# A gate table in device memory, laid out by table position or by chunk of the down stage

## The chip, the cores and the metric

The kernel runs on one core of a Trainium2 chip, as one launch. The metric is the time of the launch on the device in microseconds (us), lower is better. In this text PE is the matrix engine, DVE the vector engine, ACT the scalar engine, POOL the GpSimd engine and SP the engine that only issues transfers. "PEld" in a row is PE's weight load, and "SPq" and "ACTq" are the queues of instructions of SP and ACT. A core has 16 DMA engines, which move what all queues issue.

## What is computed

One layer of a hybrid block over 512 positions of width 1024 in float32: an attention branch and a short convolution, then a retrieval over 128 x 128 = 16384 experts of one neuron each (`peer_ffn`), then a norm. The change is in the experts.

```python
top_s, top_i = lax.top_k(s, 16)                       # per head and half: 16 of 128 keys
cand_s = top_s[:, :, 0, :, None] + top_s[:, :, 1, None, :]
cand_i = top_i[:, :, 0, :, None] * 128 + top_i[:, :, 1, None, :]
best_s, best_c = lax.top_k(cand_s, 16)                # 16 of 256 pairs, 8 heads
gate = jax.nn.softmax(best_s, axis=-1)
act = gelu(einsum('nhkd,nd->nhk', expert_u[expert_idx], x))
return einsum('nhk,nhkd->nd', gate * act, expert_v[expert_idx])
```

Each token picks 128 experts. An expert's number is i * 128 + j.

## The kernel before

The 512 tokens are four blocks of 128. Three of them (384 tokens) are computed densely: every expert's activation for every token is worked out, and multiplied by a gate that is zero unless the token picked the expert. The fourth ("sparse") block is computed by fetching the picked rows. On the way from one to the other there are two tables in device memory: `expert_act` (name `hd`) with the activations, i x j x 384 tokens, and `expert_gate` (name `gd`) with the gates, in 12 batches of 32 tokens.

**Up stage**, about 500 to 1215 us, 128 steps, one for each j, of some 5.5 us. In step n PE transposes the next 128 rows of `expert_u` (line 1144) and multiplies the rows of step n (24 matmuls, line 1154) in three passes over high and low halves: ACT copies the high half `uh` out of PSUM (1238), DVE takes the low half `ul` (1412), and PE needs both for the next step. ACT then runs the gelu and writes the activations of the step to `expert_act` from its own queue (1245, 1247). The raw rows of `expert_u` stand in four buffers; SP issues the load for a buffer when its transposes are done, four steps ahead of its next use (1073).

The gates are built beside it, in three blocks of 16 groups of 8 tokens. DVE makes one-hot rows (`hot`, 1475 and 1477), ACT multiplies by the gates' high part (1269), POOL makes the low part (1381), PE multiplies the one-hots into a table of gates in PSUM (`spread`, 1181), ACT evacuates it into one of two buffers `parts` (`evac`, 1279), and POOL adds the two halves of `parts` into `grid` (`gather`, 1390). Eight such additions fill the grid, 128 keys x 32 tokens. SP then writes it to the gate table (`send`, 1084), 12 times in all, four in a block. POOL's next addition waits for the send to have landed, since there is one grid; ACT's evacuation waits for the addition of two before, since there are two `parts`.

The sparse block runs here too: POOL issues an indirect DMA for each of 128 picked rows of `expert_u` (`fetch`, 1371) into a ring of five buffers, and DVE multiplies each with the tokens (`row`, 1487), between the other tasks of a step. A table by step says how many rows DVE takes, and POOL fetches as ring buffers are freed. DVE, ACT and POOL each run a fixed order, so that a wait in front of one task holds what stands behind it.

**Down stage**, about 1220 to 1742 us, 32 chunks of four j each. For a chunk SP loads 2 MB of `expert_v` (1076), 768 KB of activations (`dh`, 1088) and 768 KB of gates (`dg`, 1091); DVE multiplies the two (1512), ACT and DVE split everything into high and low halves (1286, 1295, 1496, 1505), and PE does 72 matmuls (1213). Buffers are double, and the loads of a chunk are issued when the chunk two before has been split. DVE also adds the fetched rows of `expert_v` for the sparse block (1492). The first gate read waits until all 12 sends have landed.

Of the kernel before, what the change touches and what calls it, by code (L numbers as in the profile page):

```python
# [18 lines left out]
F = mybir.dt.float32  # L19
# [7 lines left out]
P = 128  # L27
# [10 lines left out]
KEYS = 128  # L38
# [28 lines left out]
DT = DB * P  # L67
# [849 lines left out]
G4 = 4  # L917
ROUNDS = KEYS // G4 // 2
# [74 lines left out]
def experts_program(nc, sem, psum, m, a, acc, sT, const, score, rank_of, gain, st, hd, gd, raw, u_in, u_view, ut_full, shared, out):  # L993
# [10 lines left out]
    grid = m.put("grid", 112, [P, KEYS, 32])  # L1004
# [21 lines left out]
    dg = [m.put(f"dg{i}", kb, [P, DT // 32, G4, 32]) for i, kb in enumerate((150, 174))]  # L1026
# [18 lines left out]
    S = {n: sem(n) for n in (  # L1045
        "v_half eq_hot eq_key found index_ready exp_in exp_out gate_norm sel_ready selT_full selT_in gate_split hot_eq "
        "g_evac g_sum g_out x3_ready row_used dot_act weighed").split()}
    v_part = [sem(f"v_part{i}") for i in range(2)]
    row_in = [sem(f"row_in{i}") for i in range(RING_D)]
    v_in, dg_in, dh_in, v_hi, v_lo, w_f, w_hi, w_lo, mm_done = (  # L1050
        [sem(f"d_{n}{i}") for i in range(2)] for n in ("v_in", "g_in", "h_in", "v_hi", "v_lo", "w_f", "w_hi", "w_lo", "mm_done"))
# [3 lines left out]
    uv = u_view.rearrange("i (r s) d -> i r s d", s=4)  # L1055
    vv = a["expert_v"][0].rearrange("(i r j) d -> i r (j d)", r=KEYS // G4, j=G4)
    hg = hd.rearrange("i (r j) t -> i r (j t)", j=G4)
    gv = gd.rearrange("b i (r x) -> i b r x", x=G4 * 32)
    HALF = STEPS // 2
    ORDER = {SPARSE: 0, 0: 1, 1: 2, 2: 3}  # L1060

    def experts_sync(sp_):

        for free in (*ut_full, *u_mm, *h_done, *g_full, S["g_evac"], S["g_sum"], *v_lo, *w_lo):
            sp_.sem_inc(free, PRIMED)
        for free in (*h_out, S["g_out"]):
            sp_.sem_inc(free, PRIMED * 16)

        def load(r, buffers=range(4)):
            for s in buffers:  # L1070

                sp_.wait_ge(ut_full[s % 2], r * 2 + s // 2)
                sp_.dma_start(raw[s][:].unsqueeze(1), uv[:, ds(r, 1), s, :]).then_inc(u_in[s], 16)

        def load_rows(s, at):
            sp_.dma_start(v_raw[s][:].rearrange("p j d -> p (j d)").unsqueeze(1), vv[:, at, :]).then_inc(v_in[s], 16)

        def load_part(s, j):
            sp_.dma_start(v_raw[s][:, j:j + 1, :], vv[:, s:s + 1, j * D:(j + 1) * D]).then_inc(v_part[s], 16)

        def send(q):

            sp_.wait_ge(S["g_sum"], 8 * q + 8 + PRIMED)
            sp_.dma_start(gd[:, :, :].rearrange("b p x -> p b x")[:, q:q + 1, :],
                          grid[:].rearrange("p j n -> p (j n)").unsqueeze(1)).then_inc(S["g_out"], 16)

        def load_acts(s, at):
            sp_.dma_start(dh[s][:].rearrange("p j t -> p (j t)").unsqueeze(1), hg[:, at, :]).then_inc(dh_in[s], 16)

        def load_gates(s, at):  # L1090
            sp_.dma_start(dg[s][:].rearrange("p b j n -> p b (j n)"),
                          gv[:, :, at, :].rearrange("p b o x -> p b (o x)")).then_inc(dg_in[s], 16)

        sp_.wait_ge(last_tile, tiles)
        load(0, range(3, 4))
        for r in range(1, STEPS // 4):
            load(r, range(2))
            if 4 * r - 4 in SEND:
                send(SEND[4 * r - 4])
            load(r, range(2, 4))  # L1100
            if r in AHEAD_AT:
                i = AHEAD_AT.index(r)
                if i in (0, G4):
                    sp_.wait_ge(ranked, EACH * (12 + i))
                elif i == G4 + 2:
                    sp_.wait_ge(S["selT_full"], DB)
                load_part(*divmod(i, G4))
        load_acts(0, slice(0, 1))

        sp_.wait_ge(S["g_out"], (DT // 32 + PRIMED) * 16)  # L1110
        load_gates(0, slice(0, 1))

        for s in range(2):
            sp_.wait_ge(ut_full[s], HALF + PRIMED)
        load_acts(1, slice(1, 2))
        load_gates(1, slice(1, 2))

        for s in range(2):
            sp_.wait_ge(h_out[s], (HALF + PRIMED) * 16)
        with sp_.Fori(1, ROUNDS) as r:  # L1120
            for s in range(2):

                sp_.wait_ge(w_lo[s], r + PRIMED)
                load_acts(s, ds(r * 2 + s, 1))
                load_gates(s, ds(r * 2 + s, 1))
                sp_.wait_ge(v_lo[s], r + PRIMED)
                load_rows(s, ds(r * 2 + s, 1))
        sp_.wait_ge(S["row_used"], SLOTS)
        sp_.dma_start(fnorm[:], a["final_norm"].unsqueeze(0).broadcast_to([P, D])).then_inc(Z["fn_in"], 16)
        for n, b in enumerate((SPARSE, *range(DB - 1))):  # L1130
            sp_.wait_ge(Z["normed"], n + 1)
            sp_.dma_start(out[0, b * P:(b + 1) * P, :], acc[:, b, :]).then_inc(Z["out"], 16)
        sp_.wait_ge(Z["normed"], NB)
        sp_.dma_start(out[0, (DB - 1) * P:DB * P, T:D], acc[:, DB - 1, T:D]).then_inc(Z["out"], 16)
        sp_.wait_ge(Z["out"], (NB + 1) * 16)
# [486 lines left out]
def layer(nc, a, out):  # L1622
    ctx = ExitStack()
    with ctx:
        def sem(name):
            return ctx.enter_context(nc.semaphore(name))

        psum = ctx.enter_context(nc.psum_tensor("psum", [P, 8 * T], F))
        banks = [psum[:, i * T:(i + 1) * T] for i in range(8)]
        m = Map(nc, (nc.sbuf_base + 63) // 64 * 64)  # L1630
        acc = m.put("acc", 0, [P, NB, D])
        sT = m.put("xTh", 16, [P, C, T], R), m.put("xTl", 32, [P, C, T], R)
        const = {n: m.put(n, 48 + i / 2, [P, P])
                 for i, n in enumerate(("ident", "iota", "tri", "ones", "causal", "gap"))}
        const["vecs"] = m.put("vecs", 51, [P, 32])
        score = m.put("score", 52, [P, NB, LISTS, KEYS])
        st = m.put("st", 198, [P, 5, NB])
        gain = m.put("gain", 203.75, [P, D])
        hd = nc.dram_tensor("expert_act", (P, KEYS, DT), F).ap()
        gd = nc.dram_tensor("expert_gate", (DT // 32, P, KEYS * 32), F).ap()  # L1640
        u_raw = [m.put(f"u_raw{i}", kb, [P, D]) for i, kb in enumerate((100, 104, 136, 140))]
        u_in = [sem(f"u_in{i}") for i in range(4)]
        u_view = a["expert_u"][0].rearrange("(i j) d -> i j d", j=KEYS)
        ut_full = [sem(f"ut_full{i}") for i in range(2)]
        rank_of = rank_stage(nc, sem, m, score)
        mix, *shared = mix_program(nc, sem, banks, m, a, acc, sT, const, u_raw, u_in, u_view, ut_full, score, rank_of[0], gain, st)
        experts = experts_program(nc, sem, psum, m, a, acc, sT, const, score, rank_of, gain, st, hd, gd, u_raw, u_in, u_view,
                                  ut_full, shared, out)

        with nc.Block() as block:  # L1650
            @block.sync
            def _(sp_):
                mix["sync"](sp_)
                experts["sync"](sp_)

            @block.gpsimd
            def _(pool):
                mix["gpsimd"](pool)
                experts["gpsimd"](pool)

            @block.tensor
            def _(pe):
                mix["tensor"](pe)
                experts["tensor"](pe)

            @block.scalar
            def _(act):
                last_list = mix["scalar"](act)
                experts["scalar"](act, last_list)

            @block.vector
            def _(dve):
                mix["vector"](dve)
                experts["vector"](dve)
# [21 lines left out]
```

## Time and profile before

| | us |
|---|---|
| median of 3 runs | 1747.38 |
| lowest and highest run | 1744.31, 1748.79 |
| the profiled execution | 1751.13 |
| its span, first to last instruction | 1749.1 |
| PE busy | 1709.5 (98%) |
| VectorE busy | 1293.4 (74%) |
| ScalarE busy | 774.1 (44%) |
| GpSimd busy | 768.1 (44%) |
| moved by DMA | 413.80 MB, 237 GB/s on the mean |

PE is the engine that is nearly always busy. A matmul's end is modelled in such a profile, so that busy time says little on how well it is used; its idle gaps are what another engine or a transfer costs it. A gap behind the name of an engine and a line means that the wait ended when this instruction ended. The granted clock of PE is 0.994 of full speed on the mean.

### The profile page before, as it was taken

What the parts mean: (1) busy time and instruction counts of PE and PEld (TensorE: products, weight loads), DVE (VectorE), ACT (ScalarE), POOL (GpSimd) and SP (SyncE); (2) the same over time, 40 slices, a digit from 0 to 9 for tenths busy, and PEclk for the clock granted to TensorE, in tenths of its full rate; (3) what the DMA queues carried; (4) which work ended last, traced back from release to release, by engine and by line L of the source; (5) the groups of instructions that cost most, each with busy time, mean ns of one, the idle gap of its engine ahead of it and who ended that gap; (6) DMA issues with size and microseconds to landing.
All of it is one profiled execution on the core that took longest, in us unless ns stands there. A gap on an engine that the chain in (4) does not pass through costs nothing.

```text
span 1749.1 us, 24587 instructions
## 1 busy us (share of the span) xinstructions
PE 1709.5 (98%) x9066; PEld 1520.8 (87%) x9066; DVE 1293.4 (74%) x1838; ACT 774.1 (44%) x1101; POOL 768.1 (44%) x486
## 2 busy tenths in 40 slices
PE   7999999998999999999999999999999999999998
PEld 5777778887889999999999999999888888888886
DVE  2555511115999899989999789885787877878886
ACT  5454423234333566655667466654233233233233
POOL 3333234332311456564666578882433333334330
PEclk9999999999999999999999999999999999999999
DMA  5222223322235677677777988898999999999992
GB/s 157 73 62 81 72 63 94 107 73 72 80 123 202 210 243 246 239 267 259 258 246 253 331 292 295 297 311 311 377 382 373 356 376 366 359 367 369 357 382 79
DMA packets 212437, 413.80 MB, mean 237 GB/s; under 512 B 11520, under 2 KB 150816, under 8 KB 207008
## 3 DMA queue, kind: packets, MB, share of 16 engines
q1 hardware_dynamic: 156880, 253.51, 41.7%
q0 software_dynamic: 36864, 134.23, 21.4%
q10 hardware_dynamic: 18640, 25.45, 4.1%
q8 instruction: 20, 0.33, 0.1%
q14 instruction: 33, 0.27, 0.0%
HBM read 360.73 MB, written 52.43 MB: 236 GB/s over the span
## 4 chain that ended last, share of the span: by engine, by line
PE 80%; DVE 9%; POOL 3%; DMA 3%; issue 2%; ACT 2%; ACTq 0%; SPq 0%; POOLq 0%; DVEq 0%
PE psum L1213 30%; PE psum L230 22%; PE psum L1154 19%; PE psum L1144 3%; DVE ring L1487 2%; DMA ring<-in_expert_u,index 2%; DVE ul L1412 2%; PE psum L1181 2%; POOL ring L1371 1%; PE psum L304 1%; POOL grid L1390 1%; PE psum L290 1%; PE psum L424 1%; DVE hot L1475 1%; PE psum L318 1%
## 5 line engine op out<-in xcount | busy, mean ns | idle before, releaser
L1154 PE MATMUL psum<-xTh,uh 128*128 128x384 f32 x1024 | 355.0, 347 | 9.5 <-DVE ul L1412 8.8
L1154 PE MATMUL psum<-xTl,uh 128*128 128x384 f32 x1024 | 344.1, 336 | 0.0
L1154 PE MATMUL psum<-xTh,ul 128*128 128x384 f32 x1024 | 344.0, 336 | 0.0
L213 POOL TENSOR_TENSOR wl<-raw,wh 128x1024 fp32r<-128x1024 f32 x72 | 172.8, 2409 | 320.1 <-ACT wh L486 320.1
L1371 POOL DMA_INDIRECT ring<-in_expert_v,index x128 | 174.8, 1365 | 296.8 <-DVE acc L1492 253.6
L1213 PE MATMUL psum<-vh,dwh 128*128 128x512 f32 x768 | 298.9, 389 | 1.2 <-DVE dwl L1505 1.2
L1213 PE MATMUL psum<-vh,dwl 128*128 128x512 f32 x768 | 298.8, 389 | 0.0
L1213 PE MATMUL psum<-vl,dwh 128*128 128x512 f32 x768 | 298.8, 389 | 0.0
L1286 ACT ACTIVATE vh<-v_raw 128x4096 fp32r<-128x4096 f32 x31 | 112.6, 3633 | 340.2 <-PE psum L1213 339.8
L1371 POOL DMA_INDIRECT ring<-in_expert_u,index x128 | 174.1, 1360 | 150.1 <-DVE ring L1487 76.2
L1487 DVE SCALAR_TENSOR_TENSOR ring<-ring,x 128x1024 f32<-128x1024 f32 x120 | 200.1, 1679 | 18.9 <-DMA ring<-in_expert_u,index 17.4
L1154 PEld LDWEIGHTS psum<-xTh,uh 128*128 128x128 f32 x1024 | 192.8, 188 | 16.2 <-DVE ul L1412 14.8
L1496 DVE TENSOR_TENSOR vl<-v_raw,vh 128x4096 fp32r<-128x4096 f32 x31 | 137.2, 4425 | 84.3 <-ACT vh L1286 84.3
L1154 PEld LDWEIGHTS psum<-xTl,uh 128*128 128x128 f32 x1024 | 193.2, 189 | 0.0
L1154 PEld LDWEIGHTS psum<-xTh,ul 128*128 128x128 f32 x1024 | 192.8, 188 | 0.0
L1390 POOL TENSOR_TENSOR grid<-parts 128x512 f32<-128x512 f32 x96 | 146.5, 1526 | 94.5 <-ACT parts L1279 67.3
L230 PE MATMUL psum<-xTh,wh 128*128 128x512 f32 x432 | 171.0, 396 | 0.9 <-POOL wl L213 0.9
L1492 DVE SCALAR_TENSOR_TENSOR acc<-ring,weight,acc 128x1024 f32<-128x1024 f32 x128 | 164.2, 1283 | 10.4
L1213 PEld LDWEIGHTS psum<-vh,dwh 128*128 128x128 f32 x768 | 144.2, 188 | 31.4 <-issue 1.5
L1213 PEld LDWEIGHTS psum<-vl,dwh 128*128 128x128 f32 x768 | 144.2, 188 | 29.9
L1213 PEld LDWEIGHTS psum<-vh,dwl 128*128 128x128 f32 x768 | 144.2, 188 | 29.9
L1412 DVE TENSOR_TENSOR ul<-psum,uh 128x1024 fp32r<-128x1024 f32 x128 | 155.6, 1216 | 18.2 <-ACT uh L1238 15.9
(209 smaller groups left out, 2893.3 us busy)
## 6 DMA issues: line engine op xcount, KB each, us to landing
u_raw<-in_expert_u SPq DMA_DIRECT2D x128, 512.0 KB
v_raw<-in_expert_v SPq DMA_DIRECT2D x30, 2048.0 KB, 12.2
expert_act<-hb ACTq DMA_DIRECT2D x128, 192.0 KB
expert_gate<-grid SPq DMA_DIRECT2D x12, 2048.0 KB, 7.5
dh<-expert_act SPq DMA_DIRECT2D x32, 768.0 KB, 4.3
dg<-expert_gate SPq DMA_DIRECT2D x32, 768.0 KB
raw<-in_w_in SPq DMA_DIRECT2D x40, 512.0 KB, 3.8
raw<-in_w_q SPq DMA_DIRECT2D x16, 512.0 KB, 3.9
```

The costliest lines, as they stand in the source:

```text
L213: nc.gpsimd.tensor_tensor(wl[slot][:], raw[slot][:], wh[slot][:].bitcast(F), ALU.subtract).then_inc(w_lo[slot], 1)
L230: done = nc.tensor.matmul(out, w[slot][:, at, :], x[:, i, :], start=(first and n == 0), stop=(last and n == 2))
L1144: last = nc.tensor.transpose(utp[s][:, c * P:(c + 1) * P], raw[n % 4][:, c * P:(c + 1) * P], ident[:])
L1154: last = nc.tensor.matmul(zb[s][:, 0:DT], w[s][:, c, :], x[:, c, 0:DT], start=(c == 0 and i == 0), stop=(c == C - 1 and i == 2))
L1213: last = nc.tensor.matmul(sums[k], w[s][:, j, b * P:(b + 1) * P], v[s][:, j, half * T:(half + 1) * T], start=(first and j == 0 and n == 0) ...
L1286: nc.scalar.activation(vh[s][:], v_raw[s][:], ACT.Copy).then_inc(v_hi[s], 1)
L1371: nc.gpsimd.indirect_dma_start(out=ring[k][:], out_offset=None, in_=tables[x // SLOTS], in_offset=bass.IndirectOffsetOnAxis(ap=index[:, x ...
L1390: nc.gpsimd.tensor_tensor(grid[:, :, n0:n0 + 4].rearrange("p k n -> p n k"), parts[x % 2][:, :, 0, :], parts[x % 2][:, :, 1, :], ALU.add). ...
L1412: nc.vector.tensor_tensor(ul[s][:].rearrange("p c f -> p (c f)"), utp[s], uh[s][:].rearrange("p c f -> p (c f)").bitcast(F), ALU.subtract) ...
L1487: nc.vector.scalar_tensor_tensor(at, at, 1.0, x3 if x < IN_UP else x3_late[:], ALU.mult, ALU.mult, accum_out=dots[:, k:k + 1]).then_inc(S[ ...
L1492: nc.vector.scalar_tensor_tensor(acc3, at, weight[:, k:k + 1], acc3, ALU.mult, ALU.add).then_inc(S["row_used"], 1)
L1496: nc.vector.tensor_tensor(vl[s][:], v_raw[s][:], vh[s][:].bitcast(F), ALU.subtract).then_inc(v_lo[s], 1)
```

## The change

The gate table's axes are put in another order. Before it was batch (12), partition i (128), then 128 keys x 32 tokens. Now it is i (128), chunk (32), batch (12), then 4 keys x 32 tokens. What the down stage reads of one partition for one chunk, 12 x 128 numbers, stands in one piece of 6 KB; before it stood in 12 pieces of 512 bytes, 2 MB apart. What a send writes from one partition, 4096 numbers of 16 KB, goes to 32 places of 512 bytes each, 6 KB apart; before it was one piece. The bytes are the same, and so are the tiles on the chip, the waits and the instructions of every engine with their order.

```diff
-    gv = gd.rearrange("b i (r x) -> i b r x", x=G4 * 32)
+    gv = gd.rearrange("i r b x -> i r (b x)")
...
         def send(q):
 
             sp_.wait_ge(S["g_sum"], 8 * q + 8 + PRIMED)
-            sp_.dma_start(gd[:, :, :].rearrange("b p x -> p b x")[:, q:q + 1, :],
-                          grid[:].rearrange("p j n -> p (j n)").unsqueeze(1)).then_inc(S["g_out"], 16)
+            sp_.dma_start(gd[:, :, q, :], grid[:].rearrange("p (r j) n -> p r (j n)", j=G4)).then_inc(S["g_out"], 16)
...
         def load_gates(s, at):
-            sp_.dma_start(dg[s][:].rearrange("p b j n -> p b (j n)"),
-                          gv[:, :, at, :].rearrange("p b o x -> p b (o x)")).then_inc(dg_in[s], 16)
+            sp_.dma_start(dg[s][:].rearrange("p b j n -> p (b j n)").unsqueeze(1), gv[:, at, :]).then_inc(dg_in[s], 16)
...
-        gd = nc.dram_tensor("expert_gate", (DT // 32, P, KEYS * 32), F).ap()
+        gd = nc.dram_tensor("expert_gate", (P, 2 * ROUNDS, DT // 32, G4 * 32), F).ap()
```

Here `P` is 128, `DT` 384, `KEYS` 128, `G4` 4 and `2 * ROUNDS` 32.

## Rows read from the trace of the kernel before

**Rows 1.** Waits of PE, whole span: total us, times, longest us.

```profile
PE psum L1154 <- DVE ul L1412: 8.8, 14, 2.7
```

**Rows 2.** Windows, down stage: us, busy us per engine (instructions), PEclk, DMA share, GB/s.

```profile
1250.00:1700.00 450.00, 450.00 (x1987) 372.72 (x1986) 365.68 (x207) 140.41 (x57) 170.95 (x126) 1.00 0.99 369
```

**Rows 3.** The tile expert_gate, whole span: who waited for it, its writes' landings.

```profile
  POOL grid L1390: 25.7, 9
...
DMA to landing us min/median/max: 6.7/7.5/12.2
```

**Rows 4.** DMA queues, 150 to 400 us, weights loading: packets, MB, share of 16 engines.

```profile
q1 hardware_dynamic: 39280, 20.97, 28.9%
```

**Rows 5.** DMA, whole span: ACT's queue; activation loads: issues, KB each, us to landing.

```profile
q10 hardware_dynamic: 18640, 25.45, 4.1%
...
dh<-expert_act SPq DMA_DIRECT2D x32, 768.0 KB, 4.3
```

**Rows 6.** Timelines of SP and DVE before the down stage: start us, us, instruction, [idle before].

```profile
1192.74 0.38 SPq L1091 DMA_DIRECT2D dg<-expert_gate  x1
...
1210.89 1.76 DVE L1512 TENSOR_TENSOR dh<-dh,dg 128x1536 f32<-128x1536 f32 x1 [0.49 <-DMA dg<-expert_gate]
```

**Rows 7.** DMA queues, 641 to 645 us, the only queue with packets there.

```profile
q1 hardware_dynamic: 110, 1.80, 107.1%
```

**Rows 8.** Timelines of SP, ACT and POOL around the first send.

```profile
640.29 0.35 SPq L1084 DMA_DIRECT2D expert_gate<-grid  x1
...
642.33 0.34 ACTq L1247 DMA_DIRECT2D expert_act<-hb  x1
...
653.83 1.02 ACT L1279 ACTIVATE parts<-psum 128x1024 f32<-128x1024 f32 x1 [0.47 <-ACT hb L1245]
...
643.63 0.98 POOL L1371 DMA_INDIRECT ring<-in_expert_u,index  x1
647.29 1.29 POOL L1390 TENSOR_TENSOR grid<-parts 128x512 f32<-128x512 f32 x1 [2.68 <-DMA expert_gate<-grid]
```

**Rows 9.** Timelines of POOL, ACT and DVE around sends 10 and 11.

```profile
1100.47 1.83 POOL L1390 TENSOR_TENSOR grid<-parts 128x512 f32<-128x512 f32 x1 [4.08 <-DMA expert_gate<-grid]
...
1104.81 1.03 ACT L1279 ACTIVATE parts<-psum 128x1024 f32<-128x1024 f32 x1 [0.47 <-ACT hb L1245]
...
1146.63 1.31 POOL L1390 TENSOR_TENSOR grid<-parts 128x512 f32<-128x512 f32 x1 [4.07 <-DMA expert_gate<-grid]
...
1149.07 1.03 ACT L1279 ACTIVATE parts<-psum 128x1024 f32<-128x1024 f32 x1 [0.47 <-ACT hb L1245]
...
1151.78 3.59 DVE L1487 SCALAR_TENSOR_TENSOR ring<-ring,x 128x1024 f32<-128x1024 f32 x1 [2.76 <-DMA ring<-in_expert_u,index]
```

**Rows 10.** DMA queues, 1201 to 1205 us: POOL's (q0) and SP's (q1).

```profile
q0 software_dynamic: 342, 1.24, 75.7%
q1 hardware_dynamic: 351, 0.18, 15.2%
```

**Rows 11.** DMA queues, 778 to 784 us, in the fourth send.

```profile
q1 hardware_dynamic: 125, 2.03, 79.8%
q0 software_dynamic: 112, 0.39, 17.2%
```

**Rows 12.** Timeline of DVE behind the fourth send.

```profile
786.70 2.64 DVE L1487 SCALAR_TENSOR_TENSOR ring<-ring,x 128x1024 f32<-128x1024 f32 x1 [2.02 <-DMA ring<-in_expert_u,index]
```

**Rows 13.** The chain that ended last, from 774 us: start us, us, what.

```profile
774.57 12.10 DMA ring<-in_expert_u,index
...
790.54 6.02 PE psum L1154 x24
797.43 4.17 PE psum L1154 x24
802.94 4.19 PE psum L1154 x24
```

**Rows 14.** Waits of PE, 785 to 1160 us: total us, times, longest us.

```profile
PE psum L1154 <- DVE ul L1412: 6.4, 6, 2.7
```

## The prediction

> **What bounds the kernel now.** I read the waits of PE first, because PE is busy for 98% of the span: what it never waits for can't make the kernel faster. Over the whole program nearly all that the expert stages lose at PE is 8.8 us in 14 waits for VectorE's ul, the low half of the transposed rows that the up stage multiplies [rows 1]. The down stage, where every gate piece is read, loses nothing: PE is busy for 450.00 of 450 us, though the DMA engines are busy too, 0.99 of the time [rows 2]. So a cheaper read of the gates has nothing to give there. Then I asked who waits for the gate table itself: POOL, 25.7 us in 9 waits before it adds new gates into the grid (L1390) [rows 3], and, once, DVE at the first read, 0.5 us [rows 6]. POOL isn't PE, so the question is what hangs on POOL and what hangs on the DMA engines while a send runs. The 12 sends are the only place where this change can reach PE.
>
> **The reads.** Each of 32 reads of 768 KB goes from 1536 pieces of 512 bytes to 128 of 6 KB. A 512-byte piece costs an engine 0.289 x 250 x 16 / 39280 = 29.4 ns [rows 4], so a read now takes 1536 x 29.4 / 16 = 2.8 us. The activations have just the new form, and land in 4.3 us by the median [rows 5]. Even a read for nothing would save at most those 2.8 us of DMA time a chunk, and by [rows 2] no part of it is on PE's path: 0. If DMA gets slack, gathers for the sparse block land sooner, for which PE doesn't wait either. At the entry of the down stage the first read is issued at 1192.74, when the last send has landed, and DVE starts with it at 1210.89 after 0.49 us of waiting [rows 6]. The new read is short, the last send longer; I expect the two to cancel within 2 us, and DVE has the other work of steps 125 and 126 there: 0, from -0.5 to +2.
>
> **The sends.** Each of 12 goes from 128 pieces of 16 KB to 4096 of 512 bytes, 256 for each DMA engine. Now: in the 4 us from 641 the SP queue's 110 packets, all of the send, took 1.071 x 4 x 16 / 110 = 0.62 us each [rows 7], so a send is 8 x 0.62 = 5.0 us of all 16 engines, and lands in 6.7 us at best, 7.5 by the median [rows 3]. New: 256 x 29.4 ns = 7.5 us. That is a price of reads; no row shows a write of 512 bytes. The nearest write is the activations' queue, 0.041 x 1749 x 16 / 18640 = 62 ns for 1.4 KB on the mean, completions included [rows 5], which lies on the line of the reads. So I take 7.5 us, +2.5 per send, with 29 ns as the low end (+2.5) and, as if each piece cost as much as one of the activations, 62 ns as the high one (15.9 us, +10.9). A gain can't be excluded by the piece's price, but by its count: nothing here moves bytes faster than the 16 KB pieces do.
> The Trainium skill (DMA: Bandwidth & Descriptors, Specifications) gives 512 bytes as the smallest transfer that still runs at line rate. By it a send would stay at 5.0 us; [rows 4, 7] say 7.5 against 5.0, and the sum goes by them.
>
> What do 2.5 us cost? **In the middle of a block** POOL waits for the send before its next addition: the send leaves at 640.29, POOL starts at 647.29 after waiting 2.68 [rows 8]. With the new send, and with one gather and one write of activations now running inside it (below), I put its landing at 10.5 us, so POOL starts near 650.8. The addition takes 1.3 us, and the one who needs it is ACT, which evacuates into the same parts buffer at 653.83 [rows 8]. 653.83 - 652.1 = 1.7 us to spare: 0 for PE, at six of nine such sends. **In the third block** the margins are smaller. POOL's additions start at 1100.47 and 1146.63, each after 4.1 us of waiting, and ACT asks at 1104.81 and 1149.07 [rows 9]: 2.5 and 1.1 us after their ends. An extra 2.5 to 3.5 us makes ACT late by up to 1 us at the first and 1.4 to 2.4 at the second, and POOL's gathers with it. PE has had slack against ACT in most of these steps, DVE being later than ACT (at 1151.78 it waits 2.76 us for a row, [rows 9]). I charge +1.5 us for the two together, 0 to +5.
>
> **What rides beside a send** is where a gain can come from. DMA engines take turns between queues piece by piece: from 1201 to 1205 the SP queue's 351 packets (mostly 512-byte pieces of the first gate read) ran beside 342 of POOL's gathers (4 KB) [rows 10]; from 778 to 784, inside the fourth send, it is 125 pieces of 16 KB beside 112 of gathers [rows 11]. One to one both times, whatever the size, and so gathers got 75.7% of the engines against 15.2% in one case, and 17.2% against 79.8% in the other. What comes while 16 KB pieces are queued also starts late: the activations issued at 642.33 and the gather issued at 643.63 [rows 8] have no packet before 645 [rows 7]. Small pieces let gathers through.
> It matters where POOL issues gathers in a row: at sends 4, 8 and 11. The gather issued at 774.57, with the fourth send, takes 12.1 us [rows 13], and DVE waits 2.02 us for it until 786.70 [rows 12]; DVE's ul comes behind it, PE idles 2.7 us, and is slow for a while after it, so that 24 matmuls take 6.02 us in place of 4.17 [rows 13]. PE's waits between 785 and 1160, 6.4 us in 6 [rows 14], are this one, three behind the eighth and the eleventh send (there DVE waits 2.76 us at 1151.78 for a row, [rows 9]), and two of 0.2 with no dense send beside them. If gathers land some 4 us sooner, as eight pieces beside 0.03 us pieces rather than 0.62 us ones would (8 x 0.6 = 4.7 us), then 6.4 - 2 x 0.2 = 6.0 us of idle time and 6.02 - 4.17 = 1.85 us of slow matmuls go: -7.8 us, from -8 to -2.
> The Trainium skill (DMA: Bandwidth & Descriptors, Queues, rings and completion order) has an engine drain a packet of some 9 to 17 descriptors of one ring before it turns to the next. By that a turn of 512-byte pieces would last 0.26 to 0.5 us against 0.62 now, and most of the gain would be missing: a sum of about -2 in place of -6.3. The counts, 351 against 342 [rows 10], speak for one piece a turn.
>
> The next u rows are queued behind the send on SP's own queue. They are asked for four steps after their issue; a step is 5.5 us (797.43 to 802.94 in [rows 13]), 22 us in all. A send that yields to five gathers (5 x 8 x 0.16 = 6.4 us) ends near 774.5 + 0.8 + 7.5 + 6.4 + 1.5 = 791, and the rows issued at about 778 land near 793, against a need near 798: covered, with 4 us left. Without that cover PE waits directly.
>
> Sum: -7.8 (gathers) + 1.5 (third block) + 0 (reads, mid-block sends) = -6.3 us against the profiled execution's 1751.1: 1744.8. That execution was 3.7 us above the median of the three runs, 1747.4; from there the same sum is **1741**.
>
> **Rivals.**
> *A: no change to be told (within 0.3%, about what a measurement of this kernel can tell from none, 5.2 us).* Gathers land sooner, but only the fourth send's stall goes (-4.5), and the third block takes +2 to +4: -2, 1745. For it: in the fourth send the queues together take all of the engines' time (79.8 + 17.2% and the activations, [rows 11]), so that the order of pieces shifts waits without removing work, and 2.5 us are added. Against it: the clear 1:1 turns.
> *B: slower, by the send's length.* The mid-block margin of 1.7 us is gone when 256 pieces take 7.5 + 1.7 = 9.2 us, at 36 ns a written piece; then ACT waits, and with it uh, ul and PE. At 62 ns the landing is 8.4 us later than by 29 ns: ACT is late by 8.4 - 1.7 = 6.7 us at six sends, by some 9 at three; PE has about 2 us to spare at each, so 6 x 4.7 + 3 x 7 = 49 us, plus slow matmuls at some: 1800. At 40 ns it is +2.8 per send, 1 us late at six sends, mostly within PE's slack, and some 3 at three: +6 after the gain above is set against it, 1753 to 1760. For it: no row prices such a write, and 4096 of them in one transfer are 2.7 times as many as in any transfer here. Against it: the writes of 1.4 KB are on the reads' line.
> *C: slower, by what is queued behind.* If descriptors of 256 pieces an engine fill SP's queue, ACT's own small write, issued 2 us after the send [rows 8], is held until the send is through; its buffer is asked again two steps later (11 us), and the u rows lose the 4 us. It decides from a send of some 13 us; +2 us for each dense send and its slow matmuls, +10 in all: 1757.
> *D: the layout doesn't do what it says,* because pieces are merged or split otherwise. The count of packets of the SP queue would show it; with sends as before: 1747.
>
> **How the numbers follow.** Forecast (a gain of 3 to 8 us) 0.46; A 0.24; B 0.17 (two thirds of it the mild one); C 0.10; D 0.03. Faster by over 0.3% needs -5.2 us: most of the forecast's share, 0.40. Within 0.3%: the rest of it, A and D, 0.34. Slower: B, C, 0.26. The range: the low end takes the whole gain of 7.8 and a scatter of runs of 2 to 3 us, 1737; the high end takes in the mild form of B and C, 1762, and leaves out the steep form of B.
>
> **What the new profile would show.** Packets over 8 KB fall by 1536, the gate sends land in 9 to 12 us rather than 7.5; POOL waits for the gate table 25.7 + 9 x 3 = 50 us or more; DVE's waits for gathered rows behind the fourth and the eleventh send (2.02 and 2.76 us) are gone, and so are PE's wait of 2.7 at 790 and the slow matmuls behind it; the down stage shows no wait of PE. Waits of ACT's evacuation for POOL's grid of more than 10 us in total would speak for B, waits of PE or ACT for DMA for C. I would be wrong on the mechanism if gathers beside a send still take 10 us and more to land.

## The result: slower by 0.5%, where 0.4% faster was forecast

| | before | after |
|---|---|---|
| median of 6 runs, us | 1747.08 | 1757.09 |
| lowest and highest | 1742.72, 1748.79 | 1752.40, 1759.37 |
| ratio | | 1.0053 [1.0040, 1.0067] |
| the profiled execution | 1751.13 | 1753.90 |
| its span | 1749.1 | 1752.2 |

The medians are 10 us apart, the two profiled executions only 2.8: that of before lies above all six of its timed runs, that of after near the fast end of its own. Part of this stands ahead of the experts, where the change does nothing: from 200 to 400 us the granted clock was 0.96 in the trace of before and 0.98 in that of after, and before's first wait of PE for ul comes at 524.32 us, after's at 523.11. From there to the first wait of PE in the down stage (until 1220.26 and 1223.28) after takes 4.2 us longer. So the traces show where some 4 us went, and the size of the rest has to come from timed experiments.

The page of after first: its head, the packets of the whole span, and the gate table's writes and reads (KB each, median us to landing).

```profile
span 1752.2 us, 24557 instructions
PE 1709.1 (98%) x9066; PEld 1520.1 (87%) x9066; DVE 1301.1 (74%) x1838; ACT 774.2 (44%) x1101; POOL 766.8 (44%) x486
...
DMA packets 214997, 413.80 MB, mean 236 GB/s; under 512 B 11520, under 2 KB 150816, under 8 KB 211104
...
expert_gate<-grid SPq DMA_DIRECT2D x12, 2048.0 KB, 11.8
...
dg<-expert_gate SPq DMA_DIRECT2D x32, 768.0 KB, 5.7
```

The layout does what it says: 12 x (4096 - 128) more pieces for the sends and 32 x (1536 - 128) fewer for the reads make +2560, and the page of before has 212437 packets. PE is busy for 1709.1 us against 1709.5: no work was added, what was lost is idle time. The waits, first those of PE over the whole span (the row of [rows 1]), then from 530 to 1230 us those of POOL and DVE for the table (the first answers to [rows 3]), of ACT for POOL, of DVE for gathered rows, and of PE for u rows.

```profile
PE psum L1152 <- DVE ul L1410: 11.6, 17, 1.8
```

```profile
POOL grid L1388 <- DMA expert_gate<-grid: 62.7, 9, 8.3
...
DVE ring L1485 <- DMA ring<-in_expert_u,index: 9.7, 7, 2.8
...
ACT parts L1277 <- POOL grid L1388: 5.8, 5, 2.6
DVE dh L1510 <- DMA dg<-expert_gate: 1.9, 1, 1.9
...
PE psum L1142 <- DMA u_raw<-in_expert_u: 0.7, 1, 0.7
```

In the same window of before these were 25.7 (POOL), 17.4 (DVE for rows), 1.7 (ACT) and 0.5 (DVE for gates). DVE waits less for its rows, as forecast, though waits of 2.80 and 2.07 us for a row now stand at 1177.03 and 1183.44, behind the eleventh send, where before had one of 2.76 at 1151.78. POOL waits 37 us more in nine places; and PE waits for ul 2.8 us more in place of 6 less. The windows of the down stage, which answer to [rows 2], show the reads:

```profile
1250.00:1700.00 450.00, 450.00 (x1987) 372.75 (x1986) 366.21 (x210) 138.49 (x56) 171.70 (x126) 1.00 0.93 369
```

The DMA engines are busy for 0.93 of the time in place of 0.99, and PE for all of it, as before.

**The sends.** First the DMA queues from 641 to 645 us, as in [rows 7]; then, from 772 to 790, those of before and, in the next fence, those of after (q0 is POOL's, q1 SP's, q10 ACT's).

```profile
q1 hardware_dynamic: 2259, 1.16, 102.6%
```

```profile
q1 hardware_dynamic: 557, 3.64, 48.5%
q0 software_dynamic: 732, 2.67, 42.8%
```

```profile
q0 software_dynamic: 1108, 4.08, 61.3%
q1 hardware_dynamic: 2353, 1.80, 30.3%
```

A written piece of 512 bytes costs 1.026 x 4 x 16 / 2259 = 29.1 ns. Around the fourth send (issued at 774.46 in before, at 775.98 in after) the gathers move 4.08 MB in place of 2.67. In after the gathers issued from 774 to 783 us land in 7.1 to 9.3 us, those issued from 978 to 988, with the eighth send, in 8.4 to 10.3. Where both queues had work their packets are again one to one: from 785 to 787 in after 198 of gathers (4 KB) and 203 of the send (512 bytes). The chain of after has no wait near it; where before had 12.10 us of a gather and 24 matmuls in 6.02 us [rows 13], it reads:

```profile
784.32 4.19 PE psum L1152 x24
788.51 0.87 PE psum L1142 x8
789.38 4.17 PE psum L1152 x24
```

**Where the time went.** After the first send, timelines of POOL, DVE and PE (start us, us, instruction, [idle before]), to be laid beside [rows 8]:

```profile
651.07 1.30 POOL L1388 TENSOR_TENSOR grid<-parts 128x512 f32<-128x512 f32 x1 [7.71 <-DMA expert_gate<-grid]
...
657.81 3.55 POOL L1388 TENSOR_TENSOR grid<-parts 128x512 f32<-128x512 f32 x2
...
657.64 2.57 DVE L1473 TENSOR_TENSOR hot<-selT,iota 128x1024 fp32r<-128x1024 f32 x1 [1.40 <-PE psum L1179]
660.13 2.31 DVE L1475 TENSOR_TENSOR hot<-selT,iota 128x1024 fp32r<-128x1024 f32 x1
...
663.51 1.21 DVE L1410 TENSOR_TENSOR ul<-psum,uh 128x1024 fp32r<-128x1024 f32 x1
...
664.77 0.44 PE L1152 MATMUL psum<-xTh,uh 128*128 128x384 f32 x1 [0.77 <-DVE ul L1410]
```

and the same pair of one-hot operations in before:

```profile
659.20 1.23 DVE L1475 TENSOR_TENSOR hot<-selT,iota 128x1024 fp32r<-128x1024 f32 x1
660.34 1.22 DVE L1477 TENSOR_TENSOR hot<-selT,iota 128x1024 fp32r<-128x1024 f32 x1
```

POOL, released 5 us later against the send's issue, still has two additions to do when DVE makes its one-hots; each of the two one-hots takes twice its 1.2 us, ul comes late, and PE stops. The plainest place is behind the second send, POOL and DVE of after:

```profile
698.64 1.31 POOL L1388 TENSOR_TENSOR grid<-parts 128x512 f32<-128x512 f32 x1
699.90 1.89 POOL L1379 TENSOR_TENSOR hot<-hot,gate_lo 128x1024 fp32r<-128x1024 f32 x1
...
698.45 3.89 DVE L888 TENSOR_TENSOR cand<-top 128x512 f32<-128x512 f32 x1
```

DVE's operation takes 0.67 us where POOL has no tensor operation beside it (665.70 in the same trace, where POOL issues a gather); here it takes 3.89, and 0.67 + 1.31 + 1.89 = 3.87: its own time and the whole of POOL's two. POOL's two keep their usual length here; elsewhere it is POOL that is held, 2.56 us at 662.78 for what takes 1.89 above, behind an operation of DVE begun at 662.36. PE idles 0.92 us for ul at 705.24. The ul operation, one of whose inputs is in PSUM, takes 1.2 us in all these lines. The Trainium skill (SBUF — State Buffer, SBUF: two separate sides) has this rule: DVE and GpSimd share a pair of ports as a lock for a whole instruction, which a DVE operation with two SBUF inputs needs against a GpSimd operation that reads SBUF. The trace agrees with the sum of 3.87; its "whichever starts first" fits the place at 662 but not the start times of this one, where DVE's record begins 0.19 us ahead of POOL's and is the long one.

The third block has another path as well. ACT's evacuations, and the chain of after behind the tenth send:

```profile
1106.71 1.03 ACT L1277 ACTIVATE parts<-psum 128x1024 f32<-128x1024 f32 x1 [2.62 <-POOL grid L1388]
...
1153.68 1.03 ACT L1277 ACTIVATE parts<-psum 128x1024 f32<-128x1024 f32 x1 [1.46 <-POOL grid L1388]
```

```profile
1091.33 12.95 DMA expert_gate<-grid
1104.42 2.21 POOL grid L1388
1106.84 0.79 issue
1107.63 1.03 ACT uh L1236
1108.69 1.23 DVE ul L1410
1109.91 3.31 DVE hot L1473
1113.22 1.14 DVE hot L1475
1114.35 2.24 DVE ring L1485 x2
1116.59 1.15 DVE ul L1410
1117.78 6.02 PE psum L1152 x24
```

Here both paths meet: the send holds POOL, POOL holds ACT, ACT's uh is late, and then a one-hot beside POOL takes 3.31 us. PE idles 1.81 us, and its next 24 matmuls take 6.02 us in place of 4.19, at a granted clock of 0.50 from 1118 to 1121: the lower of the clock's two levels, 1.2 in place of 2.4 GHz.

### The profile page after: what moved, and what is told of

It is laid out like the page before. It is cut to its first block, busy times and chain, and to the rows that moved or that the text cites. A ratio compares the mean times of both kernels' runs of the same rounds, so it can differ in the third digit from the quotient of the medians.

```text
span 1752.2 us, 24557 instructions
## 1 busy us (share of the span) xinstructions
PE 1709.1 (98%) x9066; PEld 1520.1 (87%) x9066; DVE 1301.1 (74%) x1838; ACT 774.2 (44%) x1101; POOL 766.8 (44%) x486
## 4 chain that ended last, share of the span: by engine, by line
PE 79%; DVE 10%; DMA 4%; POOL 3%; issue 2%; ACT 2%; ACTq 0%; SPq 0%; POOLq 0%; DVEq 0%
PE psum L1211 30%; PE psum L230 22%; PE psum L1152 19%; PE psum L1142 3%; DMA u_raw<-in_expert_u 2%; DVE ul L1410 2%; DVE ring L1485 2%; DVE hot L1473 2%; PE psum L1179 2%; DMA expert_gate<-grid 1%; PE psum L304 1%; DVE hot L1475 1%; PE psum L290 1%; POOL ring L1369 1%; POOL grid L1388 1%
## 5 line engine op out<-in xcount | busy, mean ns | idle before, releaser
L1152 PE MATMUL psum<-xTh,uh 128*128 128x384 f32 x1024 | 355.1, 347 | 12.3 <-DVE ul L1410 11.6
L1369 POOL DMA_INDIRECT ring<-in_expert_u,index x128 | 168.6, 1317 | 146.1 <-DVE ring L1485 71.8
L1485 DVE SCALAR_TENSOR_TENSOR ring<-ring,x 128x1024 f32<-128x1024 f32 x120 | 186.8, 1569 | 11.2 <-DMA ring<-in_expert_u,index 9.7
L1490 DVE SCALAR_TENSOR_TENSOR acc<-ring,weight,acc 128x1024 f32<-128x1024 f32 x128 | 164.2, 1283 | 10.4
## 6 DMA issues: line engine op xcount, KB each, us to landing
expert_gate<-grid SPq DMA_DIRECT2D x12, 2048.0 KB, 11.8
```

Of the source, the lines that this page charges most:

```text
L1152: last = nc.tensor.matmul(zb[s][:, 0:DT], w[s][:, c, :], x[:, c, 0:DT], start=(c == 0 and i == 0), stop=(c == C - 1 and i == 2))
L1369: nc.gpsimd.indirect_dma_start(out=ring[k][:], out_offset=None, in_=tables[x // SLOTS], in_offset=bass.IndirectOffsetOnAxis(ap=index[:, x ...
L1485: nc.vector.scalar_tensor_tensor(at, at, 1.0, x3 if x < IN_UP else x3_late[:], ALU.mult, ALU.mult, accum_out=dots[:, k:k + 1]).then_inc(S[ ...
L1490: nc.vector.scalar_tensor_tensor(acc3, at, weight[:, k:k + 1], acc3, ALU.mult, ALU.add).then_inc(S["row_used"], 1)
```

## The experiments

Each is timed beside before on the same chip; all ratios are to before. "Lateness" below means that POOL's additions come later because they wait for a send to land. A plus line is what the kernel has in place of the minus line of the kernel named.

| kernel | us | ratio and its interval | PE's waits for ul, 530 to 1230: us, times |
|---|---|---|---|
| before | 1747.08 | | 8.6, 13 |
| after | 1757.09 | 1.0053 [1.0040, 1.0067] | 11.4, 16 |
| write alone | 1755.25 | 1.0035 [1.0021, 1.0048] | 12.5, 17 |
| read alone | 1748.28 | 1.0005 [0.9996, 1.0014] | 7.4, 14 |
| after, POOL never waits | 1740.09 | 0.9955 [0.9941, 0.9968] | 2.1, 7 |
| before, POOL never waits | 1746.04 | 0.9986 [0.9975, 0.9997] | 6.3, 10 |
| before, POOL held | 1751.79 | 1.0019 [1.0009, 1.0028] | 11.9, 16 |
| pieces of 1 KB | 1746.51 | 0.9993 [0.9984, 1.0002] | 6.5, 11 |
| before, every fourth send cut | 1743.81 | 0.9976 [0.9965, 0.9986] | 4.3, 11 |
| grid in halves | 1742.10 | 0.9971 [0.9959, 0.9982] | 2.5, 8 |
| grid in halves, sends cut | 1740.73 | 0.9952 [0.9938, 0.9965] | 2.5, 8 |
| before, POOL's additions cut | 1737.26 | 0.9931 [0.9918, 0.9945] | 2.5, 8 |
| after, POOL's additions cut | 1736.21 | 0.9926 [0.9913, 0.9940] | 2.1, 7 |

The first two rows were timed together. The others were timed in three groups, each with before beside it, whose medians there were 1748.43, 1747.77 and 1748.90; so kernels of different groups are compared by their ratios.

### The write alone, and the read alone

The new sends with reads in 12 pieces of 512 bytes (against before):

```diff
-    gv = gd.rearrange("b i (r x) -> i b r x", x=G4 * 32)
+    gv = gd.rearrange("i r b x -> (i r b x)").rearrange("(b i r x) -> i b r x", i=P, r=2 * ROUNDS, x=G4 * 32)
...
+            sp_.dma_start(gd[:, :, q, :], grid[:].rearrange("p (r j) n -> p r (j n)", j=G4)).then_inc(S["g_out"], 16)
```

> The write part of the change alone: sends go out in 512-byte pieces to the new layout, and the table is read in 512-byte pieces as before, as if it still had the old layout (so the gates reach wrong experts). Theory 1 (the longer send makes POOL's additions late, and they then fall on VectorE's one-hots and delay ScalarE's evacuations) and theory 2 (what is queued behind 4096 pieces comes late) both expect the whole loss: 8 to 12 us slower than before, a POOL wait for the table of about 60 us in all. Theory 3 (the reads, at the entry of the down stage or in it) expects less than 3 us.

The old sends with reads in one piece of 6 KB (against before):

```diff
-    gv = gd.rearrange("b i (r x) -> i b r x", x=G4 * 32)
+    gv = gd.rearrange("b i x -> (b i x)").rearrange("(i r x) -> i r x", i=P, r=2 * ROUNDS)
...
+            sp_.dma_start(dg[s][:].rearrange("p b j n -> p (b j n)").unsqueeze(1), gv[:, at, :]).then_inc(dg_in[s], 16)
```

> The read part alone: sends go out in 16 KB pieces as before, and the table is read in 6 KB pieces, as if it had a layout by partition (so the gates reach wrong experts). Theories 1 and 2 expect no difference, within 2 us of before, and a POOL wait of 26 us. Theory 3 expects most of the 10 us.

Write alone 1755.25, 1.0035; read alone 1748.28, 1.0005. The read is worth nothing that can be told, and the sends carry the loss, though 6.8 us of it against the 8 to 12 expected. Whether the write alone costs less than the whole change is not settled: the intervals meet.

### POOL without its wait for the send

After, with the sends copying a buffer that is at rest, so that POOL need not wait:

```diff
-            sp_.dma_start(gd[:, :, q, :], grid[:].rearrange("p (r j) n -> p r (j n)", j=G4)).then_inc(S["g_out"], 16)
+            sp_.dma_start(gd[:, :, q, :], acc[:].rearrange("p b d -> p (b d)").rearrange("p (r x) -> p r x", x=G4 * 32)).then_inc(S["g_out"], 16)
...
-            if x % 8 == 0 and x:
-
-                pool.wait_ge(S["g_out"], (x // 8 + PRIMED) * 16)
```

> The changed kernel with the link from send to POOL cut: each send copies 16 KB per partition of another tile that nobody writes then (the token rows, so the gate table holds no gates), in the same 4096 pieces to the same places, and POOL adds into the grid without waiting for a send. The transfers stay, POOL's wait goes. Theory 1 expects the loss gone: 1740 to 1747 us. Theory 2 expects it to stay: 1754 to 1759.

The same in before, with its 16 KB pieces:

```diff
-                          grid[:].rearrange("p j n -> p (j n)").unsqueeze(1)).then_inc(S["g_out"], 16)
+                          acc[:].rearrange("p b d -> p (b d)").unsqueeze(1)).then_inc(S["g_out"], 16)
...
-            if x % 8 == 0 and x:
-
-                pool.wait_ge(S["g_out"], (x // 8 + PRIMED) * 16)
```

> The kernel before (sends and reads in its old layout, 16 KB pieces) with the link from send to POOL cut as in the run before last: sends copy another tile of 16 KB per partition that nobody writes then (so the gate table holds no gates), POOL adds into the grid without waiting. Theory 1 (POOL's lateness is what costs) expects a gain over the kernel before, since its 26 us of POOL waits go too, but VectorE still waits for rows gathered beside 16 KB pieces at the dense sends: 1742 to 1746 us, against 1740 with 512-byte pieces. If piece size costs in itself it would be under 1739, if it pays at the dense sends over 1742.

With the same pieces and the same amount of DMA traffic, 1740.09 without the wait and 1757.09 with it: POOL's wait costs 0.98%, 17 us. In before the wait costs 0.14%, 2 us. And without any lateness the small pieces are the better ones, 0.9955 against 0.9986, 5.4 us. PE's waits, small pieces first, then 16 KB pieces:

```profile
PE psum L1152 <- DVE ul L1407: 2.1, 7, 0.5
```

```profile
PE psum L1154 <- DVE ul L1409: 6.3, 10, 2.9
```

The longest wait, 2.92 us at 985.03, stands behind the eighth send, where gathers are dense; behind the fourth there are 0.64 and 0.71. With small pieces all three are gone. So the change has two parts of opposite sign: the pieces gain 5.4 us, and the longer wait of POOL costs 15 (17 less the 2 of before), 9.3 in all. The transfers themselves, and what is queued behind them, cost nothing that can be told: rival C is out.

### POOL late without small pieces

Before, with POOL held at the nine sends in the middle of a block until DVE has made the second next one-hots:

```diff
+                k = x // 2 + 2
+                if x % 32:
+                    pool.wait_ge(hot_ready[k % 2], k // 2 + 1)
```

> The kernel before, with its layout and its transfers, and one more wait: after each of the nine sends inside a block, POOL's next addition also waits until VectorE has made the second next group of one-hots, which is at 650.8 us in the profile of before, where the addition started at 647.3 (with the change it started at 651.1). Theory 1 expects the same loss as the change or most of it, 5 to 12 us, with VectorE's one-hots some 0.2 us longer on the mean. Theory 2 expects no difference, within 3 us.

1751.79, 1.0019: slower, with the table's writes as they were, though by less than the 5 to 12 us expected. The stalls in the middle of the blocks are after's own. PE and DVE of this kernel behind the second send, to be laid beside after's 698.45 and 705.24:

```profile
698.40 3.89 DVE L888 TENSOR_TENSOR cand<-top 128x512 f32<-128x512 f32 x1
...
705.18 0.44 PE L1154 MATMUL psum<-xTh,uh 128*128 128x384 f32 x1 [0.92 <-DVE ul L1415]
```

Four more come at after's places (756.96, 908.62, 960.84 and, with 1.42 us, 1112.85); those at 664, 867 and 1076 don't. Two longer ones, 1.21 us at 785.45 and 2.26 at 990.41, stand behind dense sends. It makes up 3.4 us of the 15. A hold by DVE's progress doesn't put POOL at the same moment as the send does: POOL starts 10.1 to 10.8 us after a send's issue and 8.7 after the tenth's, where after has 10.4 to 13.1, the most behind the tenth. And it makes gathers later too, for which DVE waits 27.4 us.

### Half the lateness

Pieces of 1 KB for the sends (12 x 2048 pieces), reads of 6 KB, against after:

```diff
-            sp_.dma_start(gd[:, :, q, :], grid[:].rearrange("p (r j) n -> p r (j n)", j=G4)).then_inc(S["g_out"], 16)
+            sp_.dma_start(gd[:, :, q, :], grid[:].rearrange("p (r j) n -> p r (j n)", j=2 * G4)).then_inc(S["g_out"], 16)
```

> The change with pieces of 1 KB in the sends (2048 each; chunks in pairs), and reads of 6 KB in one piece (so the gates of a pair of chunks are mixed up). A size between the two: POOL's waits for the table should come to some 40 us, between 26 and 63. Theory 1 expects a loss between those of the two kernels, 0 to 5 us over before. If the count of pieces has a threshold of its own, it is as before or as after.

1746.51, 0.9993: no change to be told. POOL's first addition starts some 9.3 us after a send's issue, between the 7 of before and the 12 of after, and waits 41.8 us in all; DVE's waits for rows are down to 7.4 us. The trace has both sides: PE's waits behind the fourth and the eighth send are gone, and there are new ones, of which those at 1107.35 (2.07 us) and 1165.76 (1.24) are the longest. Gain and loss cancel here.

### The gain alone

Before, with sends 4, 8 and 12 (those beside dense gathers, behind which a block ends) cut into four transfers with pieces of 4 KB:

```diff
+            n = 4 if q % 4 == 3 else 1
+            w = KEYS * 32 // n
+            for i in range(n):
+                sp_.dma_start(gd[:, :, i * w:(i + 1) * w].rearrange("b p x -> p b x")[:, q:q + 1, :],
+                              grid[:].rearrange("p j n -> p (j n)")[:, i * w:(i + 1) * w].unsqueeze(1)).then_inc(S["g_out"], 16)
```

> The kernel before, with only sends 4, 8 and 12 (the ends of blocks, where POOL issues gathers in a row and waits for no send) cut into four transfers with pieces of 4 KB. If 16 KB pieces hold up the gathered rows there, as the prediction had it, VectorE's waits for rows behind sends 4 and 8 shrink and the kernel gains 2 to 5 us (1743 to 1746); if only the bytes ahead matter, no difference.

1743.81, 0.9976: a gain of 4 us, with POOL's waits as before (26.7) and DVE's for rows down from 17.4 to 11.4. PE's waits behind the fourth and the eighth send are gone or 0.2 us, and 1.41 at 1150.06, behind the eleventh, stays. By the medians it is most of the 5.4. One transfer became four here as well, and the two weren't parted.

### POOL's additions cut

To tell what it is about POOL's lateness that costs, its additions are made narrow from the ninth on, 16 of 128 keys, in after and in before; POOL, ACT and every wait otherwise stay.

```diff
+            m = KEYS if x < 8 else 16
...
-            nc.gpsimd.tensor_tensor(grid[:, :, n0:n0 + 4].rearrange("p k n -> p n k"), parts[x % 2][:, :, 0, :],
-                                    parts[x % 2][:, :, 1, :], ALU.add).then_inc(S["g_sum"], 1)
+            nc.gpsimd.tensor_tensor(grid[:, 0:m, n0:n0 + 4].rearrange("p k n -> p n k"), parts[x % 2][:, :, 0, 0:m],
+                                    parts[x % 2][:, :, 1, 0:m], ALU.add).then_inc(S["g_sum"], 1)
```

> The changed kernel with POOL's additions cut to 16 of 128 keys from the ninth on (the first eight are whole, the other keys keep old gates), so that POOL is as late behind a send as with the change but hardly works in SBUF when it comes. Theory 1a (the loss is POOL's late additions running beside VectorE's one-hots and top-k steps, which then take twice as long) expects it within 3 us of the same cut made in the kernel before (next run). Theory 1b (the loss is ScalarE's evacuations waiting for the additions, and rows fetched late) expects 6 us or more over it.

> The same cut (POOL's additions on 16 of 128 keys from the ninth on, the other keys keep old gates) in the kernel before: the base for the run above. Both theories expect it faster than the whole kernel before, by 0 to 6 us, since additions also run beside VectorE there.

1736.21 and 1737.26: the layouts no longer differ (0.9926 [0.9913, 0.9940] and 0.9931 [0.9918, 0.9945]). POOL is still released late by the small pieces, 10.3 to 11.8 us after a send's issue against 6.9 to 8.4 with 16 KB pieces, with these waits of POOL and of PE in after's form:

```profile
POOL grid L1389 <- DMA expert_gate<-grid: 39.9, 9, 7.5
...
PE psum L1152 <- DVE ul L1411: 2.1, 7, 0.5
```

In before's form PE's waits are 2.5 us in 8, none over 0.5: the stalls behind dense sends are gone as well, so that no gain of small pieces hides a loss here. So a late release alone costs nothing (it is later by 2.9 us on the mean of nine sends, in the whole kernels by 4.1); it costs when POOL then has its full additions to do. The one-hots from 600 to 1180 us (count, then total us and mean ns), first of after, then of after with narrow additions:

```profile
L1473 DVE TENSOR_TENSOR hot<-selT,iota 128x1024 fp32r<-128x1024 f32 x46 | 70.1, 1524 | 24.7 <-PE psum L1179 24.7
...
L1475 DVE TENSOR_TENSOR hot<-selT,iota 128x1024 fp32r<-128x1024 f32 x46 | 68.1, 1480 | 0.0
```

```profile
L1476 DVE TENSOR_TENSOR hot<-selT,iota 128x1024 fp32r<-128x1024 f32 x46 | 57.3, 1245 | 0.0
L1474 DVE TENSOR_TENSOR hot<-selT,iota 128x1024 fp32r<-128x1024 f32 x46 | 56.3, 1223 | 39.6 <-PE psum L1179 39.2
```

In before they take 1267 and 1457 ns, with POOL's wait taken away from after 1220 and 1459. The candidate sums (L888) take 665 ns on the mean in before and 1847 in after. With narrow additions they are still long, 1317 (before's form) and 1528 (after's), and PE loses nothing by it that shows: an operation that takes longer doesn't cost by itself. The products of the gathered rows (L1485) went the other way, 1603 ns in after against 1731, and DVE is busy for only 7.7 us more over the whole program: what changed is which of its operations stand beside POOL's.

Both kernels gain 11.6 to 12.7 us over before, where 0 to 6 had been expected for before's form. POOL's full additions cost PE in before too, and by far more than the 2 us of its waits for the table. What this pair doesn't part: narrow additions shorten POOL's backlog as well as its hold on DVE, so ACT too is served sooner.

### A version faster than both

The grid as two halves of 16 tokens, each sent when it is full (24 sends of 1 MB in 8 KB pieces), while POOL fills the other; the reads then take pieces of 256 bytes:

```diff
-            if x % 8 == 0 and x:
+            h = x // 4 % 2
+            if x % 4 == 0 and x >= 8:
...
-    grid = m.put("grid", 112, [P, KEYS, 32])
+    grid = m.put("grid", 112, [P, 2, KEYS, 16])
```

> A version of the kernel before in which the grid is two halves of 16 tokens, each sent as soon as its four additions are done (24 sends of 1 MB, pieces of 8 KB), so that POOL adds into one half while the other is on its way; the reads have 256-byte pieces, 3072 for a chunk. Theory 1 expects POOL's waits for the table to go from 26 us to near 0 and the kernel to gain 4 to 8 us (1740 to 1744). Against it: small read pieces could make the down stage wait; each chunk's gate read may take 6 us instead of 2.8, for which the down stage has slack by the profile of before.

The same with each send cut into four transfers of 2 KB pieces:

```diff
+            w = KEYS * 16 // CUTS
+            for i in range(CUTS):
+                sp_.dma_start(gd[:, :, i * w:(i + 1) * w].rearrange("b p x -> p b x")[:, q:q + 1, :],
```

> The version with two half grids, and each of its 24 sends cut into four transfers with pieces of 2 KB in place of one with 8 KB. POOL waits for no send there, so only the gain of small pieces beside gathers is left to see: from 1742 to 1738 to 1741 us if it adds to that of the halves; the same 1742 if the halves had taken it already.

1742.10 (0.9971) and 1740.73 (0.9952 [0.9938, 0.9965]). POOL never waits for the table in either, and PE's waits for ul are 2.5 us in 8 in both, as in the kernels with narrow additions:

```profile
PE psum L1160 <- DVE ul L1420: 2.5, 8, 0.5
```

Two halves take POOL's wait away: with the sends cut it is 0.5% better than before and, by the ratios, 1.0% than after. Whether the cut adds to the halves is not settled: their intervals meet, and DVE waits 6.7 us for rows in both. The reads' worse form, 256 bytes, keeps the DMA engines busy for 1.05 of the time from 1250 to 1700 in place of 0.99, and PE is busy for all of it still.

## Why the prediction was wrong, term by term

The trace's own ledger can be made from PE's idle times. It names 3.2 of the 4.2 us by which after was longer from 523 to 1223 us; that the spans differ by 3.1 as well is chance.

| term | forecast, us | in the traces, us |
|---|---|---|
| gathers beside sends 4, 8, 11 | -7.8 | -7.75 |
| mid-block sends | 0 | +4.96 |
| third block | +1.5 (0 to +5) | +6.1 |
| reads and entry of the down stage | 0 (-0.5 to +2) | -0.2 |
| sum | -6.3 | +3.2 |

The first is before's 2.68 + 1.07 + 0.54 + 1.61 of waits and 6.02 - 4.17 of slow matmuls, all gone. The second is six new waits, 0.77, 0.92, 0.89, 0.41, 1.06 and 0.91. The third is 1.24 + 0.43 + 1.81 + 1.47 and 6.02 - 4.17, less 0.25 + 0.42 that before had there. The fourth is 0.72 for u rows, less 0.52 and 0.37 elsewhere.

**Right: the gain.** Its mechanism (short pieces let gathers through) and its size in the trace. By the times it is 5.4 us (the two kernels without a wait), of which cutting three sends alone gave 4. The sum of about -2 that long turns of a queue would have given is not what came. Equal counts over 4 us fit any equal number of pieces a turn, so 351 against 342 did not decide for one piece; better is before's 781 to 784 us, with 55, 55 and 54 packets of the send, the gathers and the activations, while the 8 pieces that the send has on an engine would have taken 5.0 us in one turn.

**Right: the price of a written piece,** 29.1 ns against 29.4, so rival B's steep form was out; **the reads,** nothing, shown by the run with the read alone; and D, out by the count.

**Nearly right: the landing.** POOL starts 12.0 us after the first send's issue (651.07 - 639.05), against 10.5 forecast; 10.4 to 13.1 over the nine. ACT's margin of 1.7 us was just enough: POOL's addition ended at 652.37, and ACT's evacuation began at 652.59, 13.5 us behind the send's issue as in before.

**Wrong: "0 for PE, at six of nine such sends".** The step that failed is the one which asked who needs POOL's addition and found ACT alone. That is a question about data. POOL's late work also stands beside other operations of DVE than before, and at the places shown above DVE's one-hots and candidate sums take longer by about the time that POOL works beside them. PE's slack against DVE is small, as [rows 1] had said: 14 waits of PE, all for DVE. That DVE was the bound should have made every instruction of DVE in the 10 us behind a send part of the sum, and before's own trace showed the effect, one-hots of 1267 and 1457 ns on the mean where 1.22 or 1.23 us is the plain length.

**Wrong in size: the third block,** +6.1 against +1.5, outside its own bounds. ACT waited 2.62 and 0.75 us behind the tenth send, where up to 1 was forecast, and 1.46 behind the eleventh, as forecast (1.4 to 2.4); but I let PE's slack cover it, and the one-hot of 3.31 us behind it used that slack up. POOL started 3.9 and 3.8 us later behind these two sends than in before, against 2.5 to 3.5.

**The rivals.** The outcome is nearest to B's mild form and C (1753 to 1760; C said 1757), but by neither mechanism: that the range, up to 1762, holds the time is luck. B's said that ACT is late at six mid-block sends: ACT's waits for POOL are 5.8 us in all, under the 10 that I had named. C's wait for DMA is 0.7 us of PE at 1207.55, one place. The rule that set the sign, POOL's work against DVE's, was not among the rivals.

**Open.** The medians differ by 10 us, the traces by 3; the 17 us that the wait costs by the times are 15.8 in the spans of the two traces (1752.2 and 1736.4), while the ledger names 11 of them. The starts of ACT's gelu, one in each of the 128 steps, place 14.7: from the first to the 96th, the first two blocks, after takes 529.0 us and the kernel without the wait 522.7, and from there to the last 181.9 and 173.6. A mid-block place where PE waits 0.77 to 1.06 us makes its step 1.0 to 1.3 us longer, which is part of what the ledger misses. How the 17 divide between the lengthened DVE operations and the path over ACT in the third block wasn't parted: the held kernel gives 3.4 with little of the latter (ACT waits 1.9 us for POOL), the narrow additions take both away.

## What to carry to other kernels

A transfer's landing moves not only the one who waits for it but all that this engine does afterwards; before calling that free, look up what the bounding engine does in the new time window, and whether the two slow each other when they run together. Here DVE's one-hots, made from two tiles in SBUF, took 1.2 us alone and 2.3 to 3.3 beside POOL's operations, and a candidate sum 3.9 in place of 0.7. A change of piece size has two faces: short pieces let other queues through, and lengthen the transfer itself; take the length off the path first (here with half-size buffers in turn), and the longer transfer no longer holds anyone.

## What the runs showed of the hardware

- A 512-byte piece written to device memory costs a DMA engine 29.1 ns, against 29.4 for one read; a 16 KB piece 0.62 us. A 2 MB write is 7.4 against 5.0 us of all 16 engines.
- The gather and the activations issued 2 to 3 us into the first send have no packet from 641 to 645 us with either piece size. In after the activations issued at 641.09 have their first ones from 645 on, where the write issued at 635.6, ahead of the send, had landed 1.9 us after its issue. I had put this on pieces of 0.62 us that were queued ahead, and that can't be the reason, since 29 ns pieces do the same. What is, no run here shows.
- A DVE operation with both inputs in SBUF took 3.89 us in place of 0.67 beside two of POOL's of 1.31 and 1.89 us.
- After a wait of PE of 1.81 us (after, 1117.78) and one of 2.68 (before, 790.54) the clock was granted at 0.50, the lower of its two levels (1.2 of 2.4 GHz), for about 3 us, and 24 matmuls took 6.02 us in place of 4.17. The length of the wait alone doesn't decide it: after 2.92 us (before without POOL's wait, 985.03) and 2.26 us (before with POOL held, 990.41) the granted clock stayed at 1.00, as it did after 1.06 to 1.61. What does, no run here shows.
